# Three pairs of gate and up chunks per layer as seven quarter products, with weight sums made by accumulating transfers

## The reference, cut to what matters

```
D_FF = int(math.ceil(8 * D_MODEL / 3 / 256) * 256)     # 2816
def swiglu(x, w_gate, w_up, w_down):
    return (jax.nn.silu(x @ w_gate) * (x @ w_up)) @ w_down
...
u = rms_norm(h, ffn_norm_g[i])
h = h + swiglu(u, ffn_w_gate[i], ffn_w_up[i], ffn_w_down[i])
```

## Time and profile before

| | |
|---|---|
| time, median of 3 runs | 1034.71 us (1034.55 to 1038.23) |
| span of the profiled execution | 1032.6 us |
| TensorE busy | 1020.1 us, 99% |
| VectorE busy | 639.1 us, 62% |
| ScalarE busy | 519.0 us, 50% |
| GpSimd busy | 109.9 us, 11% |
| moved by DMA | 191.68 MB, 186 GB/s over the span |

### The profile page before, as it was taken

One profiled execution on the slowest core, in us unless ns is written; L12 is line 12 of the kernel. 1 busy time (PEld: TensorE's weight loads), 2 busy tenths in 40 slices (PEclk: granted clock), 3 DMA queues, 4 the chain that ended last, 5 costly groups with the idle time before them and its releaser, 6 DMA issues.

```text
span 1032.6 us, 13504 instructions
## 1 busy us (share of the span) xinstructions
PE 1020.1 (99%) x5494; PEld 862.1 (83%) x5494; DVE 639.1 (62%) x810; ACT 519.0 (50%) x647; POOL 109.9 (11%) x90
## 2 busy tenths in 40 slices
PE   9999999999999999999999999999999999999997
PEld 8977888888888888888888888788888889999885
DVE  6986655454557667764545457676463657777564
ACT  6427534344377668653443446654544453444533
POOL 4992100000020320010000002100000000000000
PEclk9999999999999999999999999999999999999999
DMA  8866855455444532575555554655455345545521
GB/s 328 267 189 116 302 196 197 174 197 191 176 163 163 204 123 82 204 265 180 188 184 183 204 174 159 228 207 217 167 204 191 135 164 207 200 164 182 205 104 42
DMA packets 30814, 191.68 MB, mean 186 GB/s; under 512 B 3736, under 2 KB 6296, under 8 KB 8992
## 3 DMA queue, kind: packets, MB, share of 16 engines
q1 hardware_dynamic: 25632, 179.84, 48.5%
q0 software_dynamic: 2096, 7.79, 3.1%
q10 hardware_dynamic: 3024, 3.18, 1.2%
HBM read 187.58 MB, written 3.21 MB: 185 GB/s over the span
## 4 chain that ended last, share of the span: by engine, by line
PE 91%; DVE 5%; DMA 2%; issue 1%; ACT 1%; POOL 0%; SPq 0%; ACTq 0%; POOLq 0%; DVEq 0%
PE bank L303 74%; PE bank L289 4%; PE bank L291 4%; PE bank L290 4%; DVE bank L1684 4%; PE bank L339 2%; DMA raw<-in_ws 1%; PE bank L428 1%; PE bank L643 0%; DMA u_scr<-arena 0%; PE bank L740 0%; PE bank L777 0%; DVE arena L1664 0%; ACT arena L1284 0%; DVE bank L1679 0%
## 5 line engine op out<-in xcount | busy, mean ns | idle before, releaser
L1479 DVE TENSOR_TENSOR w_lo<-raw,w_hi 128x2048 fp32r<-128x2048 f32 x157 | 360.3, 2297 | 209.7 <-ACT w_hi L991 209.5
L991 ACT ACTIVATE w_hi<-raw 128x2048 fp32r<-128x2048 f32 x168 | 321.1, 1911 | 166.0 <-PE bank L303 146.7
L303 PE MATMUL bank<-w_hi,x_hi 128*128 128x512 f32 x800 | 220.6, 397 | 0.2
L303 PE MATMUL bank<-w_lo,x_hi 128*128 128x512 f32 x800 | 214.5, 390 | 0.0
L303 PE MATMUL bank<-w_hi,x_lo 128*128 128x512 f32 x800 | 214.4, 390 | 0.0
L303 PEld LDWEIGHTS bank<-w_hi,x_lo 128*128 128x128 f32 x800 | 150.2, 188 | 32.3
L303 PEld LDWEIGHTS bank<-w_lo,x_hi 128*128 128x128 f32 x800 | 150.2, 188 | 31.9
L303 PEld LDWEIGHTS bank<-w_hi,x_hi 128*128 128x128 f32 x800 | 144.9, 188 | 31.6 <-issue 3.9
L303 PE MATMUL bank<-w_hi,z_hi 128*128 128x512 f32 x320 | 94.0, 393 | 0.1
L303 PE MATMUL bank<-w_lo,z_hi 128*128 128x512 f32 x320 | 92.8, 389 | 0.0
L303 PE MATMUL bank<-w_hi,z_lo 128*128 128x512 f32 x320 | 92.8, 389 | 0.0
(11 more groups left out here) (246 smaller groups left out, 966.3 us busy)
## 6 DMA issues: line engine op xcount, KB each, us to landing
raw<-in_ws SPq DMA_DIRECT2D x168, 1024.0 KB, 4.8
arena<-u_scr ACTq DMA_DIRECT2D x16, 142.0 KB, 4.7
arena<-in_rows POOLq DMA_DIRECT2D x2, 1024.0 KB, 5.5
toep<-bias_row POOLq DMA_DIRECT2D x1, 1536.0 KB, 34.9
h<-in_x_tok SPq DMA_DIRECT2D x2, 512.0 KB, 4.0
raw<-in_ws SPq DMA_DIRECT2D x2, 512.0 KB, 8.0
arena<-in_rows POOLq DMA_DIRECT2D x2, 512.0 KB, 4.8
arena<-toep POOLq DMA_DIRECT2D x1, 1024.0 KB, 10.6
```

The source lines that it names most:

```text
L303: ins = pe.matmul(dst, tok(a_part, k, t), w_part[:, s, c], start=first and j == 0 and i == 0, stop=last and j == 2 and i == len(ks) - 1)
L991: act.activation(w_hi[:, g % SPLIT, :], raw[:, g % RAW, :], ACT.Copy).then_inc(hi_done, 1)
L1479: dve.tensor_tensor(w_lo[:, g % SPLIT, :], raw[:, g % RAW, :], w_hi[:, g % SPLIT, :].bitcast(F32), ALU.subtract).then_inc(lo_done, 1)
```

## The change

**Pairs.** Chunks (2, 3), (5, 6) and (8, 9) of each layer are made as pairs. A pair is the product of a 2x2 arrangement of input quarters A (token tile by input half) with a 2x2 arrangement of weight pieces B (input half by chunk). Eight quarter products would be needed; Winograd's form of Strassen's algorithm takes seven:

- from A11, A12 and A22 themselves: `p1` = A11 B11, `p2` = A12 B21, `p4` = A22 T3;
- from four sums of quarters of x (`q_f32` 0 to 3): `p5` = Q0 T1, `p6` = Q1 T2, `p3` = Q2 B22, `p7` = Q3 T4;
- with T1 = B11 + B12, T4 = B12 + B22, T2 = T1 + B22, T3 = T2 + B21. The combinations are partly added in PSUM (`p6`, `p7` and `p4` go on in the bank of `p1`, `p3` in the bank of `p5`), partly in three tiles `c_11`, `c_22`, `c_12` in SBUF, copied out by ScalarE and combined by VectorE.

**Weight sums.** T1, T4 and T2 lie in three slots of `sums` (T3 takes T2's slot). GpSimd issues, for each pair, three loads (B11, B12, B22) and three transfers that add to what is there: B12 to T1, B22 to T4, and the finished T1 to T2. B21 is added by VectorE (`third_sum`). Each sum is split into high and low parts like a piece: seven splits for a pair in place of four. B12 is no longer loaded by SyncE.

**Input sums.** GpSimd makes the four sums of quarters (`input_sums`), ScalarE their high part, GpSimd the low part. The gained x of both layers now lies whole in `x_f32`, under the slot of T4; the four sums lie under the slot of T1.

**Order.** `FFN_ORDER` replaces `gu_at` and `down_at`: chunks 0, 1, pair, 4, pair, 7, pair, 10, with two down pieces inside each pair. There are three buffers of hidden values in place of one. VectorE's wait for the bias adds stands before the first `h_split`. The area for software descriptors is set to 8192.

```diff
+STEPS = (0, 1, (2, 3), 4, (5, 6), 7, (8, 9), 10)
+WITHIN = {(2, 3): (0, 1), (5, 6): (2, 4), (8, 9): (5, 7)}
+BEHIND = {4: (3,), 7: (6,), 10: (9, 8, 10)}
+TURNED = {(2, 3): (1, None), (5, 6): (2, 4), (8, 9): (5, 7), 1: (0,), 4: (3,), 7: (6,), 10: (9,)}
...
+        FFN_ORDER += [(_step, "B11"), (_step, "T1"), (_step, "T2"), (_step, "B22"), ("down", WITHIN[_step][0]),
+                      (_step, "B21"), (_step, "T4"), ("down", WITHIN[_step][1]), (_step, "T3")]
...
                 if g >= RAW:
-                    lo_ready(sp, g - RAW)
+                    old = PIECES[g - RAW]
+                    lo_ready(sp, old)
...
+                            if old == ffn_at(layer, p, "B22"):
+                                sum_there(sp, layer, p, "T2")
+                            if old == ffn_at(layer, p, "B21"):
+                                sum_there(sp, layer, p, "T3")
...
+            def product(key, o, a_hi, a_lo, b, start, release):
+
+                pe.wait_ge(hi_done, o + 1)
+                begin(b)
+                for j, (a_part, w_part) in enumerate(((a_hi, w_hi), (a_lo, w_hi), (a_hi, w_lo))):
+                    if j == 2:
+                        lo_ready(pe, o)
+                    for k in range(4):
+                        ins = pe.matmul(banks[b][:, :], a_part[:, k, :], w_part[:, o % SPLIT, k * 512:(k + 1) * 512],
...
+                    if n == NPAIR * layer + 1:
+                        pe.wait_ge(S("q_lo"), layer + 1)
+                    b1, b2, b4 = 0, 2, 1
...
+                    product(("p1", n), ffn_at(layer, p, "B11"), *of_x(0, t0), b1, True, (S("c_11"), 2 * n - 1))
+                    hidden_job(turned[0])
+                    product(("p5", n), ffn_at(layer, p, "T1"), *of_q(0), b4, True, (S("c_22"), 2 * n - 1))
+                    product(("p6", n), ffn_at(layer, p, "T2"), *of_q(1), b1, False, (S("c_12"), 2 * n - 1))
...
+                    product(("p3", n), ffn_at(layer, p, "B22"), *of_q(2), b4, False, (S("c_12"), 2 * n))
+                    down(within[0])
+                    product(("p2", n), ffn_at(layer, p, "B21"), *of_x(1, t0), b2, True, (S("c_11"), 2 * n))
+                    product(("p7", n), ffn_at(layer, p, "T4"), *of_q(3), b1, False, (S("c_22"), 2 * n))
+                    down(within[1])
+                    product(("p4", n), ffn_at(layer, p, "T3"), *of_x(1, t1), b1, False, (S("hidden"), MADE_NO[layer, one, 1]))
...
+                    if i:
+                        lo_ready(pool, ffn_at(layer, PAIRS[i - 1], "T1"))
+                        sum_there(pool, layer, PAIRS[i - 1], "T2")
+                    else:
+                        pool.wait_ge(S("q_lo"), layer + 1)
+                    pool.dma_start(sums[:, 0, :], ws[PIECE_OF[ffn_at(layer, p, "B11")]]).then_inc(S("t1_in"), 16)
...
+                    pool.dma_start(sums[:, 2, :], b12).then_inc(S("t4_in"), 16)
+                    if i:
+                        lo_ready(pool, ffn_at(layer, PAIRS[i - 1], "T3"))
+                    pool.dma_start(sums[:, 1, :], ws[PIECE_OF[ffn_at(layer, p, "B22")]]).then_inc(S("t2_in"), 16)
+                    pool.wait_ge(S("t1_in"), 32 * n - 16)
+                    pool.dma_start(sums[:, 0, :], b12, accum_op=ALU.add).then_inc(S("t1_in"), 16)
+                    pool.wait_ge(S("t4_in"), 32 * n - 16)
+                    pool.dma_start(sums[:, 2, :], ws[PIECE_OF[ffn_at(layer, p, "B22")]], accum_op=ALU.add)                         .then_inc(S("t4_in"), 16)
+                    pool.wait_ge(S("t2_in"), 16 * n)
+                    pool.wait_ge(S("t1_in"), 32 * n)
+                    pool.dma_start(sums[:, 1, :], sums[:, 0, :], accum_op=ALU.add).then_inc(S("t2_sum"), 16)
```

More of the change, by code:

```diff
@@ L49, in gu_at, with ffn_at @@
-def gu_at(i):
-    return 0 if i == 0 else 2 + 6 * ((i - 1) // 2) + 2 * ((i - 1) % 2)
-def down_at(q):
-    return 2 + 6 * q + 4
+    G[_name] = NOP
+    NOP += _n
+def ffn_at(layer, *key):
+    return G[f"ffn{layer}"] + FFN_AT[key]
+SUM_OF_OP = {ffn_at(layer, p, name): (layer, p, name) for layer in range(2) for p in PAIRS
+             for name in ("T1", "T2", "T3", "T4")}
+PIECES = [o for o in range(NOP) if o not in SUM_OF_OP]
+NPIECE = len(PIECES)
+PIECE_OF = {o: p for p, o in enumerate(PIECES)}
@@ new lines, with pair_no @@
+B12_ROW = {(layer, p): NPIECE + NPAIR * layer + i for layer in range(2) for i, p in enumerate(PAIRS)}
+SUM_SLOT = {"T1": 0, "T2": 1, "T3": 1, "T4": 2}
+def pair_no(layer, p):
+    return NPAIR * layer + PAIRS.index(p) + 1
+MADE = []
+for _layer in range(2):
+    for _step in STEPS:
+        if isinstance(_step, tuple):
+            MADE += [(_layer, _step[1], 0), (_layer, _step[0], 0), (_layer, _step[1], 1), (_layer, _step[0], 1)]
+        else:
+            MADE += [(_layer, _step, t) for t in range(TT)]
@@ L457, in ffn @@
-                for i in range(GU):
-                    token_chunk(("gu", layer, i), g0 + gu_at(i), x_hi, x_lo, ready=ready_from(m) if i == 0 else None,
-                                release=lambda t: (S("hidden"), 2 * (GU * layer + i) + t + 1),
-                                between=(lambda: hidden_job(i - 1)) if i else None,
-                                hooks=later(m, 1) if i == 0 else {})
-                    if i >= 2 and i % 2 == 0:
-                        down(i // 2 - 1)
-                down(5)
+                            ins = pe.transpose(banks[t_bank][:, k * SEQ + t * P:k * SEQ + (t + 1) * P],
+                                               hids[i % 3][:, t, k * P:(k + 1) * P], ident[:, :])
@@ L466, in ple @@
+                for step in STEPS:
+                    if isinstance(step, tuple):
+                        pair(step)
+                    else:
+                        single(step)
             def ple(layer, m):
@@ L1072, in ffn @@
+                for step in STEPS:
+                    if isinstance(step, tuple):
+                        pair(step)
+                    else:
+                        single(step)
                 scaled_hi(m + 1, 0, 0, gname)
                 scaled_hi(m + 1, 0, 1, gname)
-                feed(g0 + 35)
+                feed(G[f"ple{layer}"] + 2)
                 h_stats(m + 1, 0)
@@ L1597, in ffn @@
+                dve.wait_ge(S("r_done"), m + 1)
+                for step in STEPS:
+                    if isinstance(step, tuple):
+                        pair(step)
+                    else:
+                        single(step)
                 add_h(("ffn", layer, 0, 0), 0, 0)
```

364 lines of the change are left out of this document (272 added, 92 removed).

## The result

| | before | after |
|---|---|---|
| time, median | 1034.66 us (1034.55 to 1038.23) | 1098.44 us (1096.12 to 1099.84) |
| ratio to before | | 1.0608, 95% interval 1.0587 to 1.0629 |
| span of the profiled execution | 1032.6 us | 1094.1 us |

The kernel became 63.8 us slower. The forecast was 1073 with a range of 1036 to 1122: the direction and the range held, and 25 us of the loss were missing.

The account below looks back on a forecast made before the run. The prediction took TensorE alone to bound the feed-forwards. Its sum was 1034.7 - 16.4 (matmuls) + 44 (first pairs) + 6 (later pairs) + 0 (VectorE, ScalarE) + 5 (clock) = 1073 us, range 1036 to 1122.

Parts of the forecast that it names:

- What bounds the kernel: In the feed-forwards TensorE alone bounds; a matmul removed shortens the run by its own time until something else comes late.
- the matmuls removed: Six pairs take seven quarter products in place of eight: 72 matmuls fewer at 0.228 us, 16.4 us saved.
- First pair, 44 us: Each layer's first pair waits for T1 and T2, whose transfers start at 129: 22 us lost per layer, 44 for both.
- the 7 to 10 named as a sign: Sign of being right in the profile after: the T1 accumulate lands in 7 to 10 us.
- Later pairs, 6 us: In the four later pairs T2 has 3 us to spare, SyncE's loads may take 8: 1.5 us each, 6 in all.
- My own sign for being wrong: In the profile after, gaps at every pair would refute the forecast and mean a time above 1100 us.
- Rival 3: Slow accumulates make later pairs late too: 1154 us at 10.6 us of moving each, about 1115 at 8; chance 0.20.
- Twice the moving time for an accumulate: An accumulating transfer reads old content and addend, so it moves for 5.2 us where a load takes 2.6.
- The floor (rival 1): Accumulates land like plain loads, and neither clock nor later pairs cost anything: 1038 us; chance 0.12.
- rival 2: First-pair sums come in time, break-even with T1 at 135.9, so the kernel gets faster, 1018 to 1032 us; chance 0.10.
- VectorE and ScalarE, 0 us: Inside a pair that has its sums, VectorE (92% busy) and ScalarE keep up with TensorE: 0 us lost.
- Clock, 5 us: Stalls of 10 to 20 us lower TensorE's clock, so a product takes double once or twice: 5 us for two layers.

Follow-up runs that it names:

- x11_best: x10_first with the transposes of chunks 8 and 10 at each layer's end one down piece ahead of the down piece needing them: 1027.30 us, ratio 0.9919.
- x5_poolsums: The changed kernel with GpSimd adding T1 and T2 itself in place of two of the three accumulating transfers: 1074.12 us, ratio 1.0371.
- x9_t4last: The changed kernel with, in later pairs, T1's accumulate issued early and T4's behind T2's sum: 1074.54 us, ratio 1.0376.
- x2_accfirst: The changed kernel with, in later pairs, the accumulates of T1 and T4 both issued ahead of T2's load: 1096.48 us, ratio 1.0584.
- x10_first: x9_t4last with first-pair loads early, T1 and T2 there added by GpSimd, chunk 1's Silus before T1's splits, toep transfers later: 1035.81 us, ratio 1.0015.

## Why the prediction was right or wrong, point by point

**What bounds the kernel, and the matmuls removed: right.** 72 fewer, products at 2.73 us. The 16.4 us follow from these two numbers; no version here runs without waits. `x11_best` keeps 7.4 of them.

**First pair, 44 us: right in mechanism, 4.9 short in size.** The trace gives 25.3 and 24.6, together 49.9, of which 1.0 is slow clock that was not hidden, so 48.9 against 44. The accumulates' moving time and the single queue were right: from the real issue at 132.25 my walk gives 161.1 for T2; it was there at 162.0. The start was not: 129 taken, 132.25 measured, for a chunk 1 that ended 1 us late. The row factor ended 2.2 us late, behind two toep issues that waited for that table's write (112.44), and two of the four adds took 3.29 and 3.21 in place of the 1.27 that I took for each. My allowance of 0.9 for GpSimd and VectorE was too small. The T1 accumulate landed after 12.9 us in both layers, not in the 7 to 10 named as a sign; in layer 0 two loads, T4's accumulate and a piece of SyncE's moved beside it. Row and rule here: the second add began 0.16 us behind VectorE's low split (117.19 to 119.48) and ended at 120.64, 1.2 us after it, its own time alone. The Trainium skill, "SBUF — State Buffer", section "SBUF: two separate sides", says that the port pair of the two engines is an exclusive lock for the whole instruction when VectorE has two SBUF inputs and GpSimd reads SBUF. The trace agrees, here and in the 5.93 and 6.07 us splits of `x5_poolsums` and `x11_best`.

**Later pairs, 6 us: the step that failed.** Measured in the trace: 14.6 us of waits and 5.7 of longer third products (4.58, 3.00, 4.47 and 4.57 us in place of 2.73; the three long ones at a lower clock); by `x9_t4last` 23.9 us. I had T2 at L + 21, wanted at L + 24, and took 1.5 for each pair, though I had written that SyncE's loads may take 8. They took them: L was at 185.7, T2 at 213.85, L + 28, at a DMA share of 1.00 throughout, with 3.70 MB of SyncE's in it. Three us of spare against 8 of load should have been a loss of 4 to 5 a pair. It was not the number of accumulates: `x9_t4last` has the same ones. With T1's accumulate issued early, the place of T4's decides, wanted last and queued ahead of T2's load or sum (`x2_accfirst` against `x9_t4last`). My own sign for being wrong, gaps at every pair, came true; the time that I tied to it, above 1100, did not. Rival 3 had the place, but as its cause accumulates of 8 to 10.6 us of moving, which no stretch shows.

**Twice the moving time for an accumulate: right** (5.2 taken, 4.9 us by the rate of 213 GB/s). The trace went from 432 to 213 GB/s at the same share, a factor of 2.03. The rule that was weighed, of the Trainium skill, "Collectives: The Full Stack", section "The bandwidth ceiling: the fold count and why AG ≠ RS ≠ AR", has 1.93 for its two source reads. The trace agrees with the factor; no run here shows the reads themselves. The floor (rival 1) fell with the measured rate. For rival 2 T1 had to be there at 135.9; it came at 150.6.

**VectorE and ScalarE, 0 us: right within pairs.** No wait for VectorE's splits there is longer than 0.4 us. But I walked a pair only. The end of the layer, where the transposes of chunks 8 and 10 stand right ahead of their down pieces, cost 7.2 us by the trace and 8.5 by `x11_best`, and stood nowhere in my sum; it was in the order that I printed (`BEHIND`, `TURNED`).

**Clock, 5 us: near in size, in other places.** I tied it to standings of 10 to 20 us. Behind those the first products took 4.38 and 5.26 us in place of 2.73, 4.2 us in all, but about 3.2 of that was hidden behind T2 and only 1.0 reached the time. What did reach it lies behind waits of 3 to 4 us in the later pairs, 5.4 of the 5.7 us there. That the total, 6.4, is near 5 is luck.

In all, by the versions: 23.9 for the later pairs, 38.7 for the first ones, 8.5 for the ends, 9.0 of smaller waits and slow clock that `x11_best` still has. Together 80.1, less 16.4 is the loss of 63.8. Since each of these versions is built on the one before, they sum up by construction; the 9.0 is what is left over. Term by term by the trace: 48.9 for the first pairs, 14.9 for the later ones, 6.4 for the clock and 7.2 for the ends, 77.4 in all. By the prediction: 44 + 6 + 5 + 0 = 55.

## What to carry to other kernels

Where spare time in a queue is less than what a neighbour may take from it, price the neighbour in full: 3 us of slack under 8 us of other traffic is a loss, not a rounding. Order the transfers of one queue by when each is wanted, and issue the first ones before the stage that needs them; with the Silus ahead of T1's splits that turned a loss of 6% into the old time (`x10_first`), and the end of the layer gave the gain of 0.8% (0.6 to 1.0). And walk the end of a loop as closely as its middle, since work removed elsewhere does not help a chain that was just in time.
